# The input projection of two consecutive blocks in one pass over w_in, with the program unrolled

## What is computed

```python
proj = rmsnorm(x, norm_mix_g) @ w_in                  # 1024 -> 2816 columns
ya, wkv_new, shift_new = rwkv_group(proj[..., :P_A], ...)   # P_A = 1792; needs the row before each row
yc, v_rows = chunk_mlp(proj[..., P_A:], ...)          # the other 1024 columns, through gelu
x = x + jnp.concatenate([ya, yc], axis=-1) @ w_out
x = x + peer_ffn(rmsnorm(x, norm_ffn_g), peer_wq, peer_subkeys, peer_u, peer_v)
gate = jax.nn.sigmoid((rmsnorm(x, norm_ple_g) @ ple_gate_w).astype(jnp.float32))
x = x + ((p @ ple_w) * gate).astype(x.dtype)          # and a final rmsnorm
```

## Time and profile before

| What | us |
|---|---|
| Median of three executions | 4069.53 |
| Profiled execution, its own time | 4059.65 |
| Span in the profile of it | 4057.9 |
| Handoff to iteration 1 (its px copy, L1662) | 280.1 |
| Handoff to iterations 2, 3, 4 | 717.2, 1176.7, 1630.4 |
| Handoff to iterations 5, 6, 7 | 2084.5, 2539.0, 2996.3 |
| Handoff to iteration 8 | 3446.3 |

### The profile page before, as it was taken

The page is one execution under the profiler, slowest core; times in us unless marked ns, Lnnn a source line. Parts: engine busy times, 40 slices in busy tenths (PEclk is TensorE's granted clock), DMA queues, the critical chain, the costliest instruction groups (busy, mean ns, idle before and its releaser), DMA issues.

```text
span 4057.9 us, 42806 instructions
## 1 busy us (share of the span) xinstructions
PE 3001.7 (74%) x11794; PEld 1710.7 (42%) x11794; DVE 3009.5 (74%) x6485; ACT 866.6 (21%) x1753; POOL 2408.2 (59%) x2129
## 2 busy tenths in 40 slices
PE   6757788778776787778776787778776777753776
PEld 3743455336542455335532455336532455211431
DVE  2458876789569886789578876789579976788582
ACT  1111211322121311321121312221121212220112
POOL 1017775677556774577556774677556774575541
PEclk8778889989999899989999899989899899986778
DMA  5069999999999999999999999999999999998975
GB/s 163 31 222 389 348 362 384 398 375 354 376 347 416 349 370 373 374 372 359 374 360 416 347 372 360 385 369 363 365 354 416 341 377 369 372 351 307 357 273 209
DMA packets 453893, 1399.82 MB, mean 345 GB/s; under 512 B 44129, under 2 KB 55681, under 8 KB 453650
## 3 DMA queue, kind: packets, MB, share of 16 engines
q0 software_dynamic: 297216, 1082.26, 69.6%
q1 hardware_dynamic: 156434, 314.66, 21.0%
HBM read 1386.84 MB, written 9.93 MB: 344 GB/s over the span
## 4 chain that ended last, share of the span: by engine, by line
DVE 32%; PE 31%; DMA 16%; issue 12%; ACT 5%; PEld 2%; POOL 1%; DVEq 0%; SPq 0%; ACTq 0%; PEldq 0%; POOLq 0%
PE peer_acc L1038 10%; DVE uring L1737 7%; DMA wbuf<-in_peer_wq_dram 5%; PE bank L795 4%; DMA wbuf<-in_w_in_dram 4%; DVE accv L1730 4%; DMA wbuf<-in_w_out_dram 3%; PE bank L900 2%; PE bank L953 2%; DMA vring<-in_peer_v_dram,eidx 2%; PE bank L951 2%; PEld bank L900 1%; PE bank L955 1%; PE bank L756 1%; PE bank L1015 1%
## 5 line engine op out<-in xcount | busy, mean ns | idle before, releaser
L700 POOL DMA_INDIRECT uring<-in_peer_u_dram,eidx x1024 | 1193.2, 1165 | 947.1 <-issue 532.9
L712 POOL DMA_INDIRECT vring<-in_peer_v_dram,eidx x1024 | 1183.9, 1156 | 606.1 <-PE peer_acc L1038 306.3
L1038 PE MATMUL peer_acc<-vring,dg 128*128 128x512 f32 x2368 | 1229.2, 664 | 375.6 <-ACT dg L1086 340.2
L1737 DVE CUSTOM_DVE_ANT_0 uring<-uring,px 128x1024 f32<-128x1024 f32 x1024 | 1239.9, 1222 | 52.5 <-DMA uring<-in_peer_u_dram,eidx 21.1
L1038 PEld LDWEIGHTS peer_acc<-vring,dg 128*128 128x128 f32 x2368 | 473.8, 211 | 964.1 <-issue 641.1
L795 PE MATMUL bank<-wbuf,xT 128*128 128x512 f32 (+3 forms) x1440 | 665.1, 606 | 195.3 <-DMA wbuf<-in_w_in_dram 117.9
L1730 DVE SCALAR_TENSOR_TENSOR accv<-vring,pact,accv 128x1024 f32<-128x1024 f32 x424 | 545.2, 1286 | 71.9 <-DMA vring<-in_peer_v_dram,eidx 44.3
L795 PEld LDWEIGHTS bank<-wbuf,xT 128*128 128x128 f32 (+1 forms) x1440 | 262.9, 191 | 591.1 <-issue 279.0
L900 PE MATMUL bank<-xT,wbuf 128*128 128x128 f32 (+1 forms) x2304 | 299.8, 289 | 60.7 <-DMA wbuf<-in_peer_wq_dram 58.1
L900 PEld LDWEIGHTS bank<-xT,wbuf 128*128 128x128 f32 x2304 | 292.3, 208 | 85.0 <-DMA wbuf<-in_peer_wq_dram 68.9
L1086 ACT ACTIVATE dg<-ident,pact 128x128 f32<-128x128 f32 x592 | 200.4, 392 | 507.3 <-DVE pact L1718 498.7
(11 more groups left out here) (296 smaller groups left out, 3229.6 us busy)
## 6 DMA issues: line engine op xcount, KB each, us to landing
wbuf<-in_w_in_dram SPq DMA_DIRECT2D x198, 512.0 KB, 10.8
wbuf<-in_peer_wq_dram SPq DMA_DIRECT2D x144, 512.0 KB, 9.6
wbuf<-in_w_out_dram SPq DMA_DIRECT2D x72, 512.0 KB, 10.5
wbuf<-in_ple_gate_w_dram SPq DMA_DIRECT2D x72, 512.0 KB, 7.0
uring<-in_peer_u_dram,eidx POOLq DMA_INDIRECT x1024, 7.5
vring<-in_peer_v_dram,eidx POOLq DMA_INDIRECT x1024, 7.6
wbuf<-in_ple_w_dram SPq DMA_DIRECT2D x18, 512.0 KB, 12.3
ms<-in_shift_mu_dram SPq DMA_DIRECT2D x9, 896.0 KB, 12.0
```

What stands on the lines that cost most here:

```text
L700: gp.indirect_dma_start(uring[:, s, :], None, peer_u, expert_rows(n, j)).then_inc(sig(f"u{s}_full"), 16)
L712: gp.indirect_dma_start(vring[:, s, :], None, peer_v, expert_rows(n, j)).then_inc(sig(f"v{s}_full"), 16)
L1038: last = mm(acc[c][:, :], dg[:, n % 2, at, :], vring[:, s, c * 512:(c + 1) * 512], start=(n + at == 0), stop=(n == UNITS - 1 and j == pe_e ...
L1737: v.tensor_tensor_reduce(out=uring[:, s, :], in0=uring[:, s, :], in1=px[:, :], scale=1.0, scalar=0.0, op0=ALU.mult, op1=ALU.add, accum_out ...
```

## The change

Blocks 1 and 2, 3 and 4, 5 and 6, 7 and 8 are pairs. The front of an odd block (`paired`) forms the projection of both: it loads `x` of the next block into `x_b` (in `xm`), norms and turns it (`normB`, `turnB`, `xTB`), and `stream_both` multiplies each piece of `w_in` with both, into two banks. ACT evacuates the second result to two buffers in `ft`, and SP stores it to `in_s` in memory, six stores. The front of an even block (`spilled`) has no norm, no turning and no `win` stages: its tail part loads `in_s` into `pa` and `uv` in two loads. The embedding and the final gain of that iteration go to `ft` and `z` instead of `uv` and `pa`. The even blocks get a share table of their own (83 of 128 experts for PE), and the choice stages of the block before weigh 1.5 times as much there. By the changed weights, `lora` stands behind expert 41.7 of an odd block and 26.1 of an even one (23.8 of the sample block). The loop of iterations 2 to 7 is written out. The diff, cut to its core:

```diff
-PE_SHARE = {0: 2, 3: 1, 9: 3, 13: 2, 26: 4}
+PE_SHARE = {"full": {0: 2, 3: 1, 9: 3, 13: 2, 26: 4}, "spilled": {0: 2, 6: 3, 11: 2, 25: 4}}
...
+def paired(i):
+    return i in (1, 3, 5, 7)
+def spilled(i):
+    return i in (2, 4, 6, 8)
...
+PAIR_STAGES = ["normB", "turnB", "xTB"]
+OWN_STAGES = ["norm", "turn", "xT"] + [f"win{c}" for c in range(6)]
...
+def stage_weight(name, i=1):
+    return plain_weight(name) * (1.5 if spilled(i) and name in LATE else 1)
...
+    in_s = scratch("in_s", (P, PA + D))
...
-            with eng.Fori(2, NB) as i:
+            for i in range(2, NB):
                 iteration(i, True, True)
...
+            def store_b(i, c):
+                b, k = count(i, f"bw{c}")
+                hold(sig(f"bank{b}_read"), k + 1)
...
+                sp.dma_start(in_s[0:n, c * WC:c * WC + w], kept(c)[0:n, 0:w]).then_inc(sig(f"kept{c % 2}_stored"), 16)
...
+                if spilled(i):
+                    hold(sig("kept0_stored"), 48 * (i // 2))
+                    hold(sig("kept1_stored"), 48 * (i // 2))
+                    sp.dma_start(pa[0:size(i), :], in_s[0:size(i), 0:PA]).then_inc(sig("in_loaded"), 16)
+                    sp.dma_start(uv[0:size(i), :], in_s[0:size(i), PA:PA + D]).then_inc(sig("in_loaded"), 16)
...
+            def stream_both(i, c, n, nb, after=None):
+                own, other = take(pe, i, f"win{c}"), take(pe, i, f"bw{c}")
...
+                        last = mm(own[0:n, 0:w_c], xT[:, k, 0:n], w[:, j, :], start=(k == 0), stop=(k == KT - 1))
+                        last_b = mm(other[0:nb, 0:w_c], xT_b[:, k, 0:nb], w[:, j, :], start=(k == 0), stop=(k == KT - 1))
...
+            def keep_b(i, c):
+                pair, n = (i - 1) // 2, size(i + 1)
+                wait_pos(act, sig(f"kept{c % 2}_stored"), 16 * (3 * pair + c // 2))
...
+                    evac(i, f"bw{c}", kept(c)[0:n, 0:w], w, n, ACT.Copy if c < 3 else ACT.Gelu)
...
             def half(i, g):
                 yield f"h{g}_turn"
+                if i >= 2:
+                    act.wait_ge(sig("y_stored"), 16 * (i - 1))
+                if paired(i):
+                    act.wait_ge(sig("kept0_stored"), 24 * (i + 1))
+                    act.wait_ge(sig("kept1_stored"), 24 * (i + 1))
...
+                    if paired(i):
+                        see(ve, i, "bw5")
+                        v.memset(sm[:, 2:4, :], 0.0)
```

More of the change, by code:

```diff
@@ L182, in stage_weight, with front_uses @@
     return STAGE_WEIGHTS[name] if name in STAGE_WEIGHTS else STAGE_WEIGHTS[name.rstrip("0123456789")]
-def uses_before(i, name, setup, tail, front, sample):
-    if not isinstance(i, int):
-        return (len(front) + len(tail)) * i + (len(setup) - 2 * len(tail) + (tail + front).index(name))
-    here = (tail if i >= 2 else []) + (front if i < NB else sample if i == NB else [])
-    before = len(setup) + len(front) * min(i, NB) + (len(sample) if i > NB else 0) + len(tail) * max(i - 2, 0)
-    return before + here.index(name)
+def front_uses(i):
+    own, both = (SAMPLE_USES, FRONT_USES)[i < NB], {}
+    for b in own:
+        mine = [use for use in own[b] if not (spilled(i) and use in _IN.get(b, []))]
+        if paired(i):
+            mine = {2: ["xB0"], 3: ["xB1"], 4: ["bw0", "bw2", "bw4"], 5: ["bw1", "bw3", "sh3", "bw5"]}.get(b, []) + [use for use in mine if use != "sh3"]
+        both[b] = mine
+    return both
+USE_AT = {}
+for b in range(6):
+    order = [("setup", use) for use in SETUP_USES[b]]
+    for i in range(NB + 3):
+        order += [(i, use) for use in (TAIL_USES[b] if i >= 2 else []) + (front_uses(i)[b] if i <= NB else [])]
+    USE_AT |= {at: (b, k) for k, at in enumerate(order)}
+PIECE_AT = {}
+for i in range(NB + 3):
+    for piece in (W_TAIL if i >= 2 else []) + ([p for p in W_FRONT if not (spilled(i) and p.startswith("win"))] if i <= NB else []):
+        PIECE_AT[i, piece] = len(PIECE_AT)
 def build(nc, a, outs):
@@ L431, in iteration @@
                 run = play(by_turns(*([tail(i)] if has_tail else []), *([late(i - 1)] if has_peer else []), front(i)), names)
-                before = [sum(stage_weight(name) for name in names[:k]) for k in range(len(names))]
-                span = before[-1] + stage_weight(names[-1])
+                before = [sum(stage_weight(name, i) for name in names[:k]) for k in range(len(names))]
+                span = before[-1] + stage_weight(names[-1], i)
                 total, done = len(names), 0
@@ L606, in tail @@
                     hold(sig("bank1_filled"), count(i, "t_xT1")[1] + 1)
-                    load_x(i)
+                    if spilled(i):
+                        sp.dma_start(last_gain(i), a["norm_final_g"].partition_broadcast(P)).then_inc(sig("fgain_loaded"), 16)
+                    else:
+                        load_x(i)
                 load_w(sp, i, "gate1")
-                if not isinstance(i, int) or i <= NB:
-                    load_w(sp, i, "win0")
+                if i <= NB:
+                    if spilled(i):
+                        if rows(i) == "p":
+                            b, k = count(i, "t_pT")
+                            hold(sig(f"bank{b}_filled"), k + 1)
+                            load_prev(i)
+                    else:
+                        load_w(sp, i, "win0")
                 hold(sig("y_ready"), j + 1)
@@ L812, in front @@
                 prompt = rows(i) == "p"
-                yield "turn"
-                pe.wait_ge(sig("xn_ready"), i + 1)
-                turn_rows(i, "xT", z, n)
-                for c in range(5):
+                if not spilled(i):
+                    yield "turn"
+                    pe.wait_ge(sig("xn_ready"), i + 1)
+                    turn_rows(i, "xT", z, n)
+                    if paired(i):
+                        yield "turnB"
+                        pe.wait_ge(sig("xn_ready"), i + 2)
+                        turn_rows(i, "xB", x_b, size(i + 1))
+                for c in range(6):
+                    if c == 5 and prompt:
+                        for k, cols in enumerate(SHIFT_COLS):
+                            yield f"shift{k}"
+                            if k == 0:
+                                pe.wait_ge(sig("prev_loaded"), 16 * i + 16)
+                                wait_in(pe, i)
+                            b = take(pe, i, f"sh{k}")
+                            settle(pe)
+                            w = cols.stop - cols.start
+                            mm(b[:, 0:w], m_back[:, :], pa[:, cols], start=True, stop=False)
+                            filled(i, f"sh{k}", mm(b[:, 0:w], ident[0:1, :], xm[0:1, cols], start=False, stop=True))
+                    if spilled(i):
+                        continue
                     yield f"win{c}"
@@ L1740, in expert @@
                     weigh(i, n - 1)
[L1741 removed]
+                if n and j in ve_experts(i, n - 1):
                     sum_v(i, n - 1, j)
```

302 lines of the change are left out of this document (184 added, 118 removed).

## The result

The kernel after takes 4102.06 us (median of six, 4087.27 to 4110.9) beside 4067.49 us for the kernel before (median of six): ratio 1.0081, 95% interval [1.0054, 1.0108]. It is slower; the forecast was 4034 us. The profiled execution took 4090.1 us, with a span of 4088.4.

A forecast was written before the change was run, and what follows sets the result against it. It took memory traffic to limit the w_in stream, with DVE, PE or DMA full in later stretches. Odd +79, even -115 and unrolling 0 gave -36 from 4069.5, say 4034 us; range 3975 to 4102, the forecast's own 4010 to 4055.

The forecast's parts named there:

- Odd iterations, +79 forecast: Win stages: second w_in matmuls make PE late instead of DMA; 18 us each for iterations 3, 5, 7, 25 for 1.
- the rest at nothing: Rest of an odd iteration: evacuations, stores, SP holds, ACT's new wait and DVE's memset, costed at 0 us.
- 1.9 us of turning: Odd win stages: turning the second block's rows, counted as PE work beside 44.1 us of matmuls.
- Even iterations, -115 forecast: Even blocks without norm, turning and w_in: 31 us less in each of three, 22 less in iteration 8.
- 10.6 MB at 394 GB/s is 27 us: Even iterations: saved traffic priced at iteration 1's rate, 27 us each; a third of 11.6 us of v sums added.
- 41 us ahead of `lora`: Even iterations: `lora` can start 41 us earlier, the upper bound of the gain if moved experts fit into air.
- moved experts are paid in full: Rival, even iterations from 1783 to 1921 us: gain 9 us instead of 31, sum +43, 4113 us; chance 0.2.
- Unrolling, 0 forecast: Loop of iterations 2 to 7 written out: the jump's 4.42 us on DVE is off the path, so 0.

The follow-up runs named there:

- e5: Changed kernel with only a quarter of the second block's w_in matmuls (two of eight per column group): 4045.83 us, ratio 0.9933 to the kernel before.
- e3: Changed kernel with the sample block's second matmuls in iteration 7 given all 128 columns instead of 8: 4092.01 us, ratio 1.0059.
- e6: Kernel before, unrolled, loading 64 KB instead of 512 per w_in piece in blocks 2, 4 and 6: 4020.21 us, ratio 0.9879.
- e12: Changed kernel with v-row gathers in even blocks fetching half of each row: 4075.53 us, ratio 1.0006.
- e9: Changed kernel with DVE's weighted v sums in even blocks adding 8 of 1024 columns: 4044.37 us, ratio 0.993.
- e14: Changed kernel with 30 of 128 v-row gathers not issued in even blocks: 4062.82 us, ratio 0.9988.
- e15: Changed kernel with both e9's thin v sums and e14's left-out gathers in even blocks: 3980.99 us, ratio 0.9806.
- e1: Kernel before with iterations 2 to 7 written out instead of looped, no pairing: 4037.07 us, ratio 0.9917.
- e11: Second run of e1, the kernel before with only its loop unrolled: 4036.27 us, ratio 0.9916.
- e13: Changed kernel with v-row gathers in even blocks fetching 64 of 128 rows: 4259.61 us, ratio 1.047.

## Why the prediction was wrong

**Odd iterations, +79 forecast, +93 measured.** PE did take the w_in stream's place, its waits for w_in went, and e5 gave that time back. That iterations 3, 5 and 1 came so near to the forecast (16.1 and 17.4 for 18, 26.1 for 25) is luck all the same. The forecast let the stretch of the w_in matmuls grow by 18 and put the rest at nothing. In iterations 3 and 5 it grew by 12, and 8 us were lost in front of it, where PE waits for the second block to be normed, turned and evacuated; of this the prediction had 1.9 us of turning as work of PE, in no term of the time. In part that came back later, 4 and 2 us. In iteration 1 the two parts are 18 and 8, and e5 gives back 12 of the 18. The other costs put at nothing were next to nothing: in the win stages of iteration 5 PE's matmuls wait 1.5 us for DVE and not for ACT's evacuations or a store. Iteration 7 was mis-sized by 15: the prediction took the sample's matmuls to cost what other records cost, and alternating 8 and 128 columns made their neighbours dearer (e3).

**Even iterations, -115 forecast, -60 measured.** This is the step that failed, and in it the choice of the row: "10.6 MB at 394 GB/s is 27 us", taken from iteration 1. Iteration 1 lacks a tail, but its time per byte is no price of a byte: bytes are worth about 6 us a block in the win stages (e6) and nothing between `lora` and the end of the merges (e12). Of the 41 us ahead of `lora` that the forecast let come free it kept 31, so 10 were left for the moved experts. In iteration 4 38.6 came free; the seven experts that moved into the stretch from `lora` to the end of the merges took 16.0, since POOL was already full there; 10.9 went behind the merges, by the estimate in the last section mostly to a lower clock of PE, which stands in no term; 3.9 came back. So 15.6 are left, half of 31. The rival "moved experts are paid in full" names that stretch and comes nearest, with 4113 us, though it too has no gain from unrolling in it; it put DVE first and named POOL's two gathers in passing, and the runs show that both hold the stretch (e9, e14, e15). The profile before had it in sight: POOL's 55.5 + 49.9 of 138 us passed for air, since the 0.3 us after each gather were not added.

**Unrolling, 0 forecast, about -34 us measured** (e1, e11). The rows at the boundary were read rightly: from the last choice to the next tail's first sum the jump costs nothing. But that was the only place looked at. Iterations 2 to 7 of e11 add up to 2703.8 us, before 2729.2. The 25 us lie in small pieces: over the six iterations 13 between `wout` and the last choice, 8 between the tail's first sum and `lora`, 6 from there to the end of the merges, and none from the last choice to the next tail's first sum (3 more). So the boundary couldn't show them.

Against the unrolled kernel, then, pairing costs: odd iterations +26.4, +17.5, +23.2 and +33.3, even ones -8.0, -13.8, -7.4 and -16.3 (lengths after less lengths of e11), in sum +55. By the totals the gain of unrolling (0.8%) hid half of what pairing costs (1.6%), so the measured time lies nearer to the forecast than the pairing earned. The version that beats both kernels is e1: unrolled, each block forming its own projection.

## What to carry to other kernels

Work moved out of a memory-bound stretch is priced in the stretch into which it falls, engine by engine: add an in-order queue's fixed step to its busy time before calling it air, and ask which engine stands next. Where a change joins two edits, run each alone; here one gained 0.8% while the other lost 1.6%. A byte saved is worth what the next engine lets it be worth, not its share of the mean bandwidth. And a length that agrees with the forecast is checked stage by stage before its mechanism is believed.

## What the runs showed of the hardware that was not expected

**A gather costs POOL a fixed time.** The mean of a v gather over the whole execution is 1117 ns in the kernel after, 1139 in e12 and 1131 in e13, where half of them move half the bytes, the latter with half the rows. The Trainium skill ("Perfetto Trace Analysis", section on what "DMA-bound" means) counts the issuing engine's own track, solid with descriptor generation, among the bounds of a DMA; e12's unchanged stretch at a share of 0.79 agrees.

**Half as many rows take longer.** In e13 the 64-row gathers go to half of the partitions. Window of e13, 1907 to 1997 us, and then its page's DMA issues:

```profile
1907.00:1997.00 90.00, 65.54 (x344) 47.56 (x342) 65.60 (x102) 13.47 (x36) 72.32 (x59) 0.92 1.03 252
```

```profile
uring<-in_peer_u_dram,eidx POOLq DMA_INDIRECT x1024, 8.1
vring<-in_peer_v_dram,eidx POOLq DMA_INDIRECT x1024, 8.0
```

The DMA engines are full (1.03) at 252 GB/s; at 0.99 the kernel after moves 373. Gathers land after 8.1 and 8.0 us instead of 6.7 and 6.8. Bytes and packets of these v gathers were halved, and engine time was not: the queue of the gathers took 70.0% of a span of 4088 us for 1082 MB in the kernel after, and 69.0% of 4252 us for 948 MB in e13 (e12, with the same 948 MB in as many packets: 64.1% of 4074). Why was not tried.

**The clock behind the merges.** In iteration 4 of the kernel after PE was granted 0.50 (1.2 GHz) from 1935 to 1953 us, after 0.98 from 1917 to 1935 with PE busy 17.23 of 18 us; DVE has 6.38 of 18 us to do meanwhile. The kernel before, between the merges and `wout`:

```profile
1921.00:1944.00 23.00, 22.88 (x192) 19.15 (x191) 15.96 (x31) 3.36 (x7) 18.60 (x15) 1.00 0.92 319
```

At the full clock 192 matmuls were through in 23 us. 18 us at half the clock are 9 at the full one, most of the 10.9 us that this stretch grew by; the `wout` stages behind it, up to the first matmul of the queries, gave back 6.8 (30.7 us where they took 37.5). Iterations 2 and 6 show about the same length (43.1 and 44.6 us); in iteration 4 of e9 the stretch took 34.2 us at a clock of 0.97. What lets the clock fall was not tried.
